# One layer of attention, state-space and expert mixture: the gated unit computed by seven half-size products per slice

## The chip, the cores and the metric

The kernel runs on one core of one Trainium2 chip. The metric is the device time of one execution in microseconds. A core has a matrix engine (PE, with its weight loads listed as PEld), a Vector engine (DVE), a Scalar engine (ACT), GpSimd (POOL) and a queue engine (SP) that here issues most DMA transfers. The on-chip memory is SBUF ("ring", "arena", "small" in the names below), and matrix results land in eight PSUM banks of 128 by 512 float32 ("bank").

## The reference, cut to what matters

256 tokens of width 1024 pass through one layer. The part that the change touches is the second branch and its merge with the first:

```
y = s5_ssm(u, ...)                                    # 256 x 512
zg = gelu(y) @ w_glu + b_glu                          # 512 x 2048
ssm_branch = zg[..., :1024] * sigmoid(zg[..., 1024:])
mixed = sigmoid(gate_a) * attn_branch + sigmoid(gate_s) * ssm_branch
x = x + mixed @ w_out                                 # 1024 x 1024
x = x + moe_swiglu(rmsnorm(x), ...)                   # 32 experts, top 4, 1024 x 2048 and 1024 x 1024 each
x = x + sigmoid(rmsnorm(x) @ w_ple_gate) * rmsnorm(p @ w_ple_proj)
```

All is float32. All 32 experts' weights, about 403 MB, are read once.

## The kernel before, in words

Everything is written out by hand, engine by engine, with semaphores between them; no scheduler moves anything. Weights pass through a ring of nine places of 2 MB. The SP queue issues their loads in one fixed order, each behind a wait for the place to be read out: the input projection (eight pieces), the attention branch, the gated unit (`("glu", 0)` and `("glu", 1)`, places 4 and 5), the output projection (`("out", 0)` and `("out", 1)`, places 6 and 7), and then the experts' pieces. Places 0, 1, 2, 8 and parts of others serve as working memory before the experts' pieces reach them. PSUM banks are handed out by one list of jobs, `order_of_banks`: a job takes the next bank once `free` says that the bank's last job has been read, and its product is announced by `full`.

The stage of the change lies between the last state-space product (job `y3`) and the output projection:

- **The gated unit (L1728).** A place holds 512 columns of the linear half and the 512 matching columns of the gate half. Job `glu{i}` (i from 0 to 7) fills one bank: 128 columns of the linear half for 256 tokens, and 128 of the gate half. A weight block of 128 by 128 is the stationary operand and `GY[:, k, :]`, 256 tokens wide, streams past it; four k are summed.
- **Its eviction.** The Scalar engine takes the sigmoid of the gate half into `SZ` (L793), Vector adds the bias and multiplies (L1167), multiplies with the branch's gate (`tt`, L961) and adds the attention branch (L1171). `mixed_set` counts the eight column blocks.
- **The output projection (L1736)** is already a seven-product scheme. Four blocks of `mixed` and four of the weights are combined: `M_SUM` on Vector (L1175 to L1180) and `W_SUM` on GpSimd (L675 to L680). Six products of 512 columns go into `outa`, `outb`, `outc`, the seventh into `out3` and `out4`. Vector adds each finished sum to `X2` (`add_product`, L1263).
- **Behind it** the second RMSNorm, the transposes (L1748), the router (L1756 to L1767, `choose`), the gather (L1784, L1787) and the first expert's up product (L1911).

A waiting instruction holds up what is behind it on its own engine only. The waits on SP that matter here: place 4 is loaded anew when `glu3` is done, place 5 when `glu7` is done, the halves of places 6, 8 and 7 as the output's products finish one by one, and the second expert's pieces (`BEHIND`) as the first expert's products read out the ring (`head_read`).

Of the kernel before, what the change touches and what calls it, by code (L numbers as in the profile page):

```python
# [5 lines left out]
P = 128  # L6
# [44 lines left out]
def order_of_banks():  # L51
# [8 lines left out]
    jobs += [f"glu{i}" for i in range(8)]  # L60
# [5 lines left out]
def hybrid_layer(nc, x, p, g_mix, w_in, g_q, g_k, w_attn, a_re, a_im, log_dt, b_re, b_im, c_re, c_im, d_skip,  # L66
# [19 lines left out]
    with ExitStack() as ctx:  # L86
# [33 lines left out]
        def spread(ap, n):  # L120
# [40 lines left out]
        SZ = area(A_X, 4, SEQ)  # L161
# [7 lines left out]
                 for at in (6, 7)]  # L169
# [61 lines left out]
        EYES2 = small[:, 448:448 + E]  # L231
# [9 lines left out]
                 "cos_times_set sin_times_set keep_set weight_set weight_full back_set gelu_set sz_set mixed_set x_again "  # L241
                 "glu_gate_in x2_sq x2_ms x2_root x2_normal xn_set xn_half w_sum m_sum prod_full prod_read router_in router_set partial_full partial_set slots_set top_set exp_set chosen_set sel_first_set "
# [19 lines left out]
                     ("glu", 0): "glu3", ("glu", 1): "glu7", ("out", 0): "out4", ("out", 1): "out4"}  # L262
# [90 lines left out]
        def turn_tables(eng, st, lo, n, tmp_at, tmp_last_at):  # L353
# [7 lines left out]
            for level in range(LEVELS):  # L361
# [7 lines left out]
                if level == LEVELS - 1:  # L369
# [6 lines left out]
                    eng.wait_ge(S["cos_times_set"], n)  # L376
                    st.did(eng.tensor_tensor(c1, c1, tmp, ALU.subtract))
                    eng.wait_ge(S["sin_times_set"], n)
# [43 lines left out]
        def _(sp):  # L422
# [63 lines left out]
            for i in (2, 0, 1, 3, 4, 5, 6, 8, 7):  # L486
                at = spot(0, i)
                piece = expert_source(i // PER_EXPERT, i % PER_EXPERT)
                if divmod(i, PER_EXPERT) in AHEAD:
                    for h in range(2):  # L490
                        at_once = h
                        if at == TURN["out", 0][0]:
                            if h == 0:
                                sp.wait_ge(S["prod_full"], 1)
                                sp.wait_ge(S["w_sum"], 4)
                            else:
                                wait_full(sp, "outb")
                        elif at == PLACES - 1:
                            sp.wait_ge(S["prod_full"], 2 + h)
                        elif h == 0:  # L500
                            wait_full(sp, "outc")
                            at_once = 1
# [8 lines left out]
                elif at in held:  # L511
                    wait_full(sp, held[at])
                if i == 3:
# [95 lines left out]
        def _(pool):  # L609
# [51 lines left out]

            wait_full(pool, "y3")
            for t in range(TB):
# [8 lines left out]
            for c in range(2):  # L672
                at, use = TURN["out", c]
                pool.wait_ge(arrived[at], 16 * (use + 1))
            pool.tensor_tensor(W_SUM[0], OUT_W[1][0], OUT_W[0][0], ALU.subtract).then_inc(S["w_sum"], 1)  # L675
            pool.wait_ge(S["w_sum"], 1)
            pool.tensor_tensor(W_SUM[1], OUT_W[1][1], W_SUM[0], ALU.subtract).then_inc(S["w_sum"], 1)
            pool.tensor_tensor(W_SUM[2], OUT_W[1][1], OUT_W[1][0], ALU.subtract).then_inc(S["w_sum"], 1)
            pool.wait_ge(S["w_sum"], 3)
            pool.tensor_tensor(W_SUM[3], OUT_W[0][1], W_SUM[1], ALU.subtract).then_inc(S["w_sum"], 1)  # L680
# [25 lines left out]
        def _(act):  # L706
# [47 lines left out]
            def last_level(table, done):  # L754

                act.wait_ge(S["pool_tables_set"], 1)
                for i in range(TILES):
                    act.activation(table[:, i, P:2 * P], table[:, i, 0:P], ACT.Copy, scale=AKC[:, i:i + 1]).then_inc(S[done], 1)

            BESIDE = {0: "u0", 1: "u1", 3: "g0", 5: "g1"}  # L760
            for s in range(PAIRS + 2):
# [8 lines left out]
                if s == 2:  # L770
                    last_level(COS, "cos_times_set")
                elif s == 3:
                    last_level(SIN, "sin_times_set")
# [15 lines left out]
            for i in range(DT):  # L789
                wait_full(act, f"glu{i}")  # L790
                if i >= 4:
                    act.wait_ge(S["mixed_set"], i - 3)
                act.activation(SZ[:, i % 4, :], ps(f"glu{i}")[:, SEQ:2 * SEQ], ACT.Sigmoid,  # L793
                               bias=PAR2[:, P_BGLU + DT + i:P_BGLU + DT + i + 1]).then_inc(S["sz_set"], 1)


            act.wait_ge(S["mixed_set"], DT)
# [9 lines left out]
            def squared(t, cols, to):  # L807
                act.activation(JUNK[:, cols], X2[:, t, cols], ACT.Square,
                               accum_out=SSQ[:, to:to + 1]).then_inc(S["x2_sq"], 1)

            def normal(t):
                act.wait_ge(S["x2_ms"], t + 1)
# [1355 lines left out]
```

## Time and profile before

| | us |
|---|---|
| median of 3 runs | 1154.44 (1154.4 to 1156.12) |
| the profiled execution's own time | 1154.22 |
| its span, first to last instruction | 1152.5 |
| PE busy in the span | 1111.7 (96%) |
| Vector, Scalar, GpSimd busy | 392.2, 171.3, 167.6 |
| moved by DMA | 440.38 MB, mean 382 GB/s |

The 1.7 us between span and time lie around the program and are taken as fixed. The chain of work that ended last is 71% PE and 26% DMA.

### The profile page before, as it was taken

How to read it: one execution, taken by the hardware profiler on the slowest of the kernel's cores; microseconds unless marked ns; L12 is line 12 of the kernel's file. 1: busy time of each engine (PE TensorE's matmuls, PEld its weight loads, DVE VectorE, ACT ScalarE, POOL GpSimd, SP SyncE). 2: the span in 40 equal slices, each digit the busy share in tenths (PEclk: the TensorE clock that was granted, in tenths of full speed). 3: DMA queues.
4: the chain of work that ended last, by engine and by line, in shares of the span. 5: the costliest groups of instructions: out<-in, count | busy, mean ns of one | idle time of the engine just before them, and what ended most of it. 6: DMA issues, size and time to landing. Idle time of an engine off the chain costs nothing.

```text
span 1152.5 us, 15678 instructions
## 1 busy us (share of the span) xinstructions
PE 1111.7 (96%) x6441; PEld 489.3 (42%) x6441; DVE 392.2 (34%) x831; ACT 171.3 (15%) x319; POOL 167.6 (15%) x187
## 2 busy tenths in 40 slices
PE   9999999999999999998999999999999999999998
PEld 4578886534333333333333333333333333333344
DVE  6558867523222222222232232121212222122226
ACT  2360112500000000000211111111111111010113
POOL 2988992100000000000000000000000000000005
PEclk9999999999999999999999999999999999999999
DMA  9934287899999999999999999999999999999991
GB/s 317 371 104 142 101 327 273 287 410 427 427 426 434 430 432 432 426 437 430 426 437 431 427 434 433 426 436 433 425 436 431 428 435 432 428 435 425 427 420 44
DMA packets 42929, 440.38 MB, mean 382 GB/s; under 512 B 9877, under 2 KB 10449, under 8 KB 24722
## 3 DMA queue, kind: packets, MB, share of 16 engines
q1 hardware_dynamic: 42306, 438.36, 90.9%
q0 software_dynamic: 480, 1.57, 0.4%
q8 instruction: 21, 0.34, 0.1%
q14 instruction: 10, 0.08, 0.0%
q10 hardware_dynamic: 112, 0.02, 0.0%
HBM read 438.89 MB, written 1.05 MB: 382 GB/s over the span
## 4 chain that ended last, share of the span: by engine, by line
PE 71%; DMA 26%; DVE 1%; issue 0%; ACT 0%; SPq 0%; DVEq 0%
PE bank L1911 26%; DMA ring<-in_w_up_dram 18%; PE bank L1965 14%; DMA ring<-in_w_down_dram 9%; PE bank L1558 7%; PE bank L1984 4%; PE bank L1575 4%; PE bank L1875 2%; PE bank L1728 2%; PE bank L1736 2%; PE bank L1776 2%; PE bank L2094 2%; PE bank L1948 1%; PE bank L2022 1%; PE bank L1952 0%
## 5 line engine op out<-in xcount | busy, mean ns | idle before, releaser
L1911 PE MATMUL bank<-ring,arena 128*64 128x512 f32 x2040 | 455.6, 603 | 17.8 <-DMA ring<-in_w_up_dram 17.6
L1911 PEld LDWEIGHTS bank<-ring,arena 128*64 128x64 f32 x2040 | 144.6, 139 | 323.5 <-issue 292.3
L1965 PE MATMUL bank<-ring,arena 128*64 128x512 f32 x1024 | 228.5, 599 | 12.4 <-DMA ring<-in_w_down_dram 11.2
L1352 DVE TENSOR_TENSOR arena<-arena,bank 128x512 f32<-128x512 f32 x128 | 79.5, 682 | 282.1 <-PE bank L1984 282.0
L1328 DVE TENSOR_SCALAR arena<-bank 128x512 f32<-128x512 f32 x32 | 22.1, 692 | 358.4 <-PE bank L1911 358.4
L694 POOL TENSOR_TENSOR ring<-ring 128x2048 f32<-128x2048 f32 x1 | 4.5, 4547 | 910.1 <-DMA ring<-in_w_ple_gate_dram 910.1
L1965 PEld LDWEIGHTS bank<-ring,arena 128*64 128x64 f32 x1024 | 74.0, 137 | 146.3 <-issue 139.2
L884 ACT ACTIVATE arena<-arena 128x512 f32<-128x512 f32 x32 | 20.2, 631 | 498.3 <-DVE arena L1328 498.3
L1558 PE MATMUL bank<-arena,ring 128*128 128x256 f32 x384 | 85.9, 382 | 0.0
L1558 PEld LDWEIGHTS bank<-arena,ring 128*128 128x128 f32 x384 | 72.0, 190 | 12.4 <-issue 3.1
L1984 PE MATMUL bank<-arena 64*128 64x512 f32 x256 | 63.5, 614 | 0.0
L1875 PEld LDWEIGHTS bank<-arena 128*128 128x128 bf16 x1488 | 45.1, 98 | 25.2 <-issue 25.2
L889 ACT ACTIVATE arena<-bank 128x512 f32<-128x512 f32 x32 | 19.1, 597 | 234.8 <-PE bank L1965 234.8
L1875 PE MATMUL bank<-arena 128*128 128x64 bf16 x1488 | 48.8, 193 | 0.0
L1575 PE MATMUL bank<-ring,arena 128*128 128x512 f32 x96 | 42.2, 595 | 0.0
L1984 PEld LDWEIGHTS bank<-arena 64*128 64x128 f32 x256 | 22.2, 186 | 40.2 <-issue 40.2
L1776 PE MATMUL bank<-arena 32*64 32x512 f32 x256 | 34.8, 613 | 0.0
L887 ACT ACTIVATE arena<-bank 128x256 f32<-128x256 f32 x64 | 21.1, 381 | 48.7 <-PE bank L1948 48.7
L1728 PE MATMUL bank<-arena,ring 128*128 128x256 f32 x128 | 27.9, 380 | 0.0
L1575 PEld LDWEIGHTS bank<-ring,arena 128*128 128x128 f32 x96 | 17.9, 190 | 21.6 <-issue 21.0
L1728 PEld LDWEIGHTS bank<-arena,ring 128*128 128x128 f32 x128 | 24.2, 190 | 3.7 <-issue 0.4
L2094 PE MATMUL bank<-ring 128*128 128x512 f32 (+1 forms) x64 | 24.5, 542 | 0.0
(278 smaller groups left out, 807.1 us busy)
## 6 DMA issues: line engine op xcount, KB each, us to landing
ring<-in_w_up_dram SPq DMA_DIRECT2D x40, 4096.0 KB, 33.2
ring<-in_w_down_dram SPq DMA_DIRECT2D x24, 4096.0 KB, 33.3
ring<-in_w_up_dram SPq DMA_DIRECT2D x38, 2048.0 KB, 25.9
ring<-in_w_down_dram SPq DMA_DIRECT2D x14, 2048.0 KB, 15.1
ring<-in_w_up_dram SPq DMA_DIRECT2D x19, 1024.0 KB, 7.7
ring<-in_w_in_dram SPq DMA_DIRECT2D x7, 2048.0 KB, 18.2
ring<-in_w_glu_dram SPq DMA_DIRECT2D x4, 1024.0 KB, 6.3
ring<-in_w_out_dram SPq DMA_DIRECT2D x2, 2048.0 KB, 8.2
```

The source lines that it names most:

```text
L1328: dve.tensor_scalar(ACTS[:, 0, :], bank[UG][:, :], LIMIT, None, ALU.min).then_inc(m["g_set"], 1)
L1352: dve.tensor_tensor(part, part, bank[at][:, :], ALU.add).then_inc(m["sc_add"], 1)
L1558: last = pe.matmul(b[:, SEQ * i:SEQ * (i + 1)], weight(key, a)[:, k, P * m:P * (m + 1)], rhs[:, k, :], start=(k == 0), stop=(k == n - 1))
L1575: last = pe.matmul(b[:, :], HT[:, k, t * P:(t + 1) * P], weight(("in", n), DT)[:, k, :], start=(k == 0), stop=(k == DT - 1))
L1728: last = pe.matmul(b[:, SEQ * h:SEQ * (h + 1)], held[:, k, h, P * (i % 4):P * (i % 4 + 1)], GY[:, k, :], start=(k == 0), stop=(k == WT - 1))
L1736: last = pe.matmul(b, of[:, k, :], w[:, k, cols], start=start and k == 0, stop=stop and k == 3, skip_group_check=True)
L1776: pe.matmul(bank[UG + w][HALF * h:HALF * (h + 1), :], PICK[rows, :], BUP[rows, :], start=True, stop=False)
L1875: last = pe.matmul(bank[GX][:, CAP * d:CAP * (d + 1)], XB[t][:, part, P * d:P * (d + 1)], SELB[:, t, :], start=(i == 0), stop=(i == 3 * TB ...
L1911: last = pe.matmul(to, XS[:, k, :], columns, start=False, stop=(k == DT - 1))
L1965: last = pe.matmul(bank[YB][HALF * c:HALF * (c + 1), :], ACTT[:, j, HALF * h:HALF * (h + 1)], piece[:, j, 512 * c:512 * (c + 1)], start=(h ...
L1984: pe.matmul(bank[at][:, :], WSELT[rows, t, :], Y[rows, :], start=True, stop=True).then_inc(m["sc_full"], 1)
L2094: last = pe.matmul(b, of[:, k, :], w[:, k, cols], start=start and k == 0, stop=(k == 3), skip_group_check=True)
```

## The change: what it does, and the diff

The gated unit is computed by seven products of half-size blocks instead of eight. For each slice s (one place, 512 linear and 512 gate columns) the rows of `y` are halved (the contraction's k = 0, 1 and k = 2, 3), the tokens are halved, and the columns are split in linear and gate. Sums of weight blocks, `G_SUM`, are made on GpSimd, sums of blocks of `y`, `Y_SUM`, on Vector. Each product covers 512 columns and 128 tokens: four column blocks of two k, so the stream past a stationary block is 128 wide instead of 256. The results pile up in the banks `ga`, `gb`, `gc`, `gd` per slice; between products the Scalar engine copies partial sums out (`held`), and Vector adds them (`linear_first`, `gate_first`, `gate_second`). The gate is opened in place in the bank (`opened`, four sigmoids of 128 columns on Scalar, one multiply on Vector), and bias, gate and attention branch are joined in the bank (`joined`, four instructions, and `mixed`). Three of the four blocks of the mixed branch stay in banks; Scalar copies them to `GATE` for the products.

Beside that: GpSimd's sums for the output come later and in another order; the re-read of x and of a bias (DMAs of GpSimd's queue) come behind the eight new sums; the load of place 4 and 5 waits for `gc0` and `gc1` (each slice's last read of its ring place by PE) and for GpSimd's last sums; the unit columns `EYES` are made before the attention; the slot numbers (`SLOT`, `LOGIT`, `RANK`, `pick`) are made behind the output's first evictions. Some semaphores are merged, which changes no order.

```diff
-    jobs += [f"glu{i}" for i in range(8)]
+    jobs += ["gc0", "gc1", "gd0", "ga0", "gd1", "gb0", "gb1", "ga1"]
...
+                    if at in (4, 5):
+                        sp.wait_ge(S["w_sum"], G_SUMS + at - 5)
...
+            for s in range(2):
...
+                glu_sum(0, s, glu_block(s, 0, 1), glu_block(s, 0, 0))
             wait_full(pool, "y3")
+            for s in range(2):
+                glu_sum(1, s, glu_block(s, 1, 1), G_SUM[0][s])
+            for s in range(2):
+                glu_sum(2, s, glu_block(s, 1, 1), glu_block(s, 0, 1))
+            for s in range(2):
+                pool.wait_ge(S["prod_full"], 3 + s)
+                glu_sum(3, s, glu_block(s, 1, 0), G_SUM[1][s])
...
+            for s in range(2):
+                linear_first(s)
+            for s in range(2):
+                gate_first(s)
+            opened("gc0", 0, 0, 1)
+            joined("gb0", 0, 0)
+            gate_second(0)
+            mixed("gb0", 0, 0)
+            gate_second(1)
+            opened("gc1", 1, 0, 2)
+            joined("gb1", 1, 0)
+            mixed("gb1", 1, 0)
+            opened("gd0", 0, 1, 3)
+            joined("ga0", 0, 1)
...
+            opened("gd1", 1, 1, 4)
+            joined("ga1", 1, 1)
+            mixed("ga1", 1, 1)
...
+            def turned_product(job, w, of, start=True):
+                b = take(job) if start else ps(job)
+                for m in range(4):
+                    for k in range(2):
+                        last = pe.matmul(b[:, P * m:P * (m + 1)], w[:, k, P * m:P * (m + 1)], of[:, k, :],
+                                         start=start and m == 0 and k == 0, stop=(k == 1), skip_group_check=True)
+                return last
...
+            for s in range(2):
+                pe.wait_ge(S["w_sum"], 7 + s)
+                wait_full(pe, f"gd{s}")
+                done(turned_product(f"ga{s}", G_SUM[3][s], y_block(1, 1), start=False), f"ga{s}")
```

**On PE**, the gated unit's end and the output's first product. Before, L1728 stands in eight pieces, one for each bank (the order counts a float32 product once; the trace lists it as two records, each with its weight load); bank0 is `glu6`, bank1 `glu7`, bank2 `outa`:

```order
L1728 MATMUL bank0<-arena,ring 128x256 [waits free0]
L1728 MATMUL bank0<-arena,ring 128x256 x7
L1728 MATMUL bank1<-arena,ring 128x256 [waits free1]
L1728 MATMUL bank1<-arena,ring 128x256 x7
L1736 MATMUL bank2<-ring,arena 128x512 [waits mixed_set,arrived6,free2]
```

After it, L1861 stands in fourteen pieces of eight; here are the last five and the output's first (bank5 is `ga0`, bank1 `ga1`, bank3 `gc1`, bank2 `outa`):

```order
L1861 MATMUL bank3<-arena,ring 128x128 [waits prod_read]
L1861 MATMUL bank3<-arena,ring 128x128 x7
L1861 MATMUL bank5<-arena,ring 128x128 [waits prod_read,w_sum,m_sum]
L1861 MATMUL bank5<-arena,ring 128x128 x7
L1861 MATMUL bank1<-arena,ring 128x128 [waits prod_read,w_sum]
L1861 MATMUL bank1<-arena,ring 128x128 x7
L1861 MATMUL bank5<-arena 128x128 [waits full4,w_sum]
L1861 MATMUL bank5<-arena 128x128 x7
L1861 MATMUL bank1<-arena 128x128 [waits full6,w_sum]
L1861 MATMUL bank1<-arena 128x128 x7
L1906 MATMUL bank2<-ring,arena 128x512 [waits mixed_in,arrived6,free2]
```

Sixty-four products of 256 columns became 112 of 128, and the last two groups wait for what Vector writes (`full4`, `full6` are `gd0` and `gd1`).

**On Vector**, before, from the last gated block to the sums for the output (bank1 is `glu7`):

```order
L1167 SCALAR_TENSOR_TENSOR arena<-bank1,small,arena 128x256 [waits sz_set]
L961 TENSOR_TENSOR arena<-arena 128x256 [waits free1]
L1171 TENSOR_TENSOR arena<-arena 128x256 [waits dve_step]
L1175 TENSOR_TENSOR arena<-arena 128x512 [waits mixed_set]
L1177 TENSOR_TENSOR arena<-arena 128x512 [waits m_sum]
L1178 TENSOR_TENSOR arena<-arena 128x512
L1180 TENSOR_TENSOR arena<-arena 128x512 [waits m_sum]
```

After it, from the opened gate of `gc0` to those sums (bank7 is `gb0`, bank0 `gb1`, bank1 `ga1`):

```order
L1273 TENSOR_TENSOR arena<-bank2,arena 128x4x128 [waits sz_set]
L1281 SCALAR_TENSOR_TENSOR bank7<-bank7,small,arena 128x128 [waits free2]
L1281 SCALAR_TENSOR_TENSOR bank7<-bank7,small,arena 128x128 x3
L1267 TENSOR_TENSOR bank4<-bank5,arena 128x512 [waits prod_full,free4]
L1287 TENSOR_TENSOR bank7<-bank7,arena 128x512 [waits dve_step]
L1267 TENSOR_TENSOR bank6<-bank1,arena 128x512 [waits prod_full,free6]
L1273 TENSOR_TENSOR arena<-bank3,arena 128x4x128 [waits sz_set]
...
L1314 TENSOR_TENSOR arena<-bank7,arena 128x512 [waits mixed_in,mixed_set,free5]
L1316 TENSOR_TENSOR arena<-arena,bank1 128x512 [waits mixed_in]
L1318 TENSOR_TENSOR arena<-arena,bank7 128x512 [waits m_sum]
L1320 TENSOR_TENSOR arena<-bank0,arena 128x512 [waits m_sum]
```

All of these read at least one operand from a bank, where before the sums for the output (L1175 to L1180) read both from the arena; between `gc0` and the sums stand twelve more instructions of 128 columns and eight more of 512, left out here.

**On GpSimd**, what stands between the last state and the output's sums, after the change:

```order
L675 TENSOR_TENSOR arena<-ring 128x1024 [waits glu_gate_in,arrived4,back_set]
L675 TENSOR_TENSOR arena<-ring 128x1024 [waits glu_gate_in,arrived5]
L675 TENSOR_TENSOR ring<-ring,arena 128x1024 [waits w_sum,full1]
L675 TENSOR_TENSOR ring<-ring,arena 128x1024 [waits w_sum]
L675 TENSOR_TENSOR ring<-ring 128x1024 x2
L675 TENSOR_TENSOR arena<-ring 128x1024 [waits prod_full,w_sum] x2
L694 DMA arena<-in_x_dram 128x1024 x2
L700 DMA arena<-in_b_up_dram 32x1024 [waits full0,free1]
L700 DMA arena<-in_b_up_dram 32x1024 x3
L701 IOTA arena 128x256
L707 TENSOR_TENSOR ring<-ring 128x2048 [waits w_sum,prod_full,arrived7,arrived6]
```

Eight sums of 1024 elements now stand ahead of the DMAs and of the four sums for the output; before, the DMAs came right behind the last state.

## Rows read from the trace of the kernel before

**Rows 1.** The page: the span in 40 slices, DMA busy in tenths
```profile
DMA  9934287899999999999999999999999999999991
```
**Rows 2.** Windows: PE, PEld, DVE, ACT, POOL busy, granted clock, DMA share, GB/s
```profile
180.00:185.00 5.00, 5.00 (x24) 4.29 (x23) 4.72 (x13) 0.84 (x3) 0.00 (x0) 1.00 0.00 0
...
210.00:215.00 5.00, 4.51 (x47) 3.12 (x46) 3.39 (x15) 2.27 (x6) 1.45 (x3) 1.00 0.36 96
...
220.00:225.00 5.00, 5.00 (x28) 1.95 (x26) 1.92 (x7) 0.60 (x3) 0.00 (x0) 1.00 0.72 261
225.00:230.00 5.00, 5.00 (x28) 1.59 (x24) 3.41 (x12) 3.32 (x3) 0.00 (x0) 1.00 1.01 364
```
**Rows 3.** Timeline of SP, the issuing queue: start, length, line, transfer
```profile
171.05 14.14 SPq L441 DMA_DIRECT2D ring<-in_w_down_dram  x2
...
220.75 0.35 SPq L540 DMA_DIRECT2D ring<-in_w_up_dram  x1
```
**Rows 4.** The chain that ended last: start, length, what
```profile
157.01 27.82 PE bank L1728 x128
184.84 20.60 PE bank L1736 x48
...
487.93 34.19 DMA ring<-in_w_up_dram
```
**Rows 5.** Chain, PE and PEld timelines, and the page's row of L1728's loads
```profile
53.26 0.87 PE bank L1625 x8
...
217.07 1.42 PEld L1787 LDWEIGHTS bank<-arena 128*128 128x128 f32 x12 [0.34 <-DVE arena L1247]
...
205.27 1.11 PE L1748 MATMUL bank<-ident,arena 128*128 128x128 f32 x8
...
L1728 PEld LDWEIGHTS bank<-arena,ring 128*128 128x128 f32 x128 | 24.2, 190 | 3.7 <-issue 0.4
```
**Rows 6.** Timeline of POOL; the last row is from the page's DMA issues
```profile
61.44 2.35 POOL L356 TENSOR_TENSOR ring<-ring,arena 128x1024 f32<-128x1024 f32 x1
...
152.78 2.80 POOL L646 TENSOR_TENSOR ring<-ring,arena 128x256 f32<-128x256 f32 x4
...
158.61 1.96 POOL L670 DMA_DIRECT2D arena<-in_b_up_dram  x4
...
160.88 4.53 POOL L675 TENSOR_TENSOR ring<-ring 128x2048 f32<-128x2048 f32 x1
...
arena<-in_x_dram POOLq DMA_DIRECT2D x2, 512.0 KB, 11.1
```
**Rows 7.** Timeline of DVE: start, length of all, line, shape
```profile
52.42 1.28 DVE L1093 TENSOR_TENSOR arena<-arena,bank 128x512 f32<-128x512 f32 x2 [4.34 <-PE bank L1575]
...
144.45 0.69 DVE L961 TENSOR_TENSOR bank<-bank,ring 128x512 f32<-128x512 f32 x1
...
157.08 0.48 DVE L1128 SCALAR_TENSOR_TENSOR arena<-arena,small,bank 128x256 f32<-128x256 f32 x1 [0.35 <-PE bank L1643]
...
161.82 3.88 DVE L961 TENSOR_TENSOR arena<-arena 128x256 f32<-128x256 f32 x1
165.74 4.63 DVE L1171 TENSOR_TENSOR arena<-arena 128x256 f32<-128x256 f32 x1
...
188.31 0.69 DVE L1177 TENSOR_TENSOR arena<-arena 128x512 f32<-128x512 f32 x1
188.92 0.69 DVE L1178 TENSOR_TENSOR arena<-arena 128x512 f32<-128x512 f32 x1
...
205.47 1.28 DVE L1263 TENSOR_TENSOR arena<-arena,bank 128x512 f32<-128x512 f32 x2 [0.45 <-PE bank L1736]
...
209.78 0.25 DVE L1228 SCALAR_TENSOR_TENSOR arena<-bank,small 128x32 f32<-128x32 f32 x1 [0.35 <-PE bank L1765]
```
**Rows 8.** Timeline of ACT
```profile
70.70 0.60 ACT L780 ACTIVATE arena<-bank 128x512 f32<-128x512 f32 x1 [2.60 <-PE bank L1558]
...
142.94 0.72 ACT L788 ACTIVATE arena<-arena 128x256 f32<-128x256 f32 x2
```

More of the change, by code:

```diff
@@ new lines, in gate_first, with gate_second @@
+            def gate_first(s):
+                wait_full(dve, f"gc{s}")
+                dve.wait_ge(S["prod_read"], 5 + s)
+                b = ps(f"gc{s}")[:, :]
+                dve.tensor_tensor(b, b, HELD_A[s], ALU.add).then_inc(S["zg_set"], 1)
+            def gate_second(s):
+                at, use = BANKS[f"gd{s}"]
+                dve.wait_ge(free[at], use)
+                dve.wait_ge(S["prod_full"], 7 + s)
+                dve.tensor_tensor(ps(f"gd{s}")[:, :], ps(f"ga{s}")[:, :], HELD_C[s], ALU.add).then_inc(full[at], 1)
@@ new lines, in opened, with joined @@
+            def opened(job, s, t, n):
+                dve.wait_ge(S["sz_set"], n)
+                part = branch_part(1, s, t)
+                release(dve.tensor_tensor(part, quarters(job), part, ALU.mult), job)
+                released(dve, job)
+            def joined(job, s, t):
+                for m in range(4):
+                    part = ps(job)[:, P * m:P * (m + 1)]
+                    i = P_BGLU + 4 * s + m
+                    st.did(dve.scalar_tensor_tensor(part, part, PAR2[:, i:i + 1], GATE[:, DT + 4 * s + m, P * t:P * (t + 1)],
+                                                    ALU.add, ALU.mult))
@@ new lines, in glu_block, with y_block @@
+            def glu_block(s, r, c):
+                return GLU_W[s][:, 2 * r:2 * r + 2, c, :]
+            def y_block(t, r):
+                return GY[:, 2 * r:2 * r + 2, P * t:P * (t + 1)]
+            pe.wait_ge(S["gelu_set"], 2)
+            pe.wait_ge(S["glu_gate_in"], 32)
+            for s in range(2):
+                arrive(("glu", s))
+                turned_product(f"ga{s}", glu_block(s, 0, 0), y_block(0, 0)).then_inc(S["prod_full"], 1)
+            pe.wait_ge(S["gelu_set"], WT)
+            for s in range(2):
+                done(turned_product(f"gb{s}", glu_block(s, 1, 0), y_block(0, 1)), f"gb{s}")
@@ new lines, in _ @@
+            pe.wait_ge(S["m_sum"], 1)
+            for s in range(2):
+                pe.wait_ge(S["w_sum"], 1 + s)
+                turned_product(f"gc{s}", G_SUM[0][s], Y_SUM[0]).then_inc(S["prod_full"], 1)
+            pe.wait_ge(S["m_sum"], 2)
+            for s in range(2):
+                pe.wait_ge(S["w_sum"], 3 + s)
+                pe.wait_ge(S["prod_read"], 1 + s)
+                turned_product(f"ga{s}", G_SUM[1][s], Y_SUM[1], start=False).then_inc(S["prod_full"], 1)
+            pe.wait_ge(S["m_sum"], 3)
@@ new lines, in _ @@
+            for s in range(2):
+                pe.wait_ge(S["prod_read"], 3 + s)
+                done(turned_product(f"gc{s}", glu_block(s, 1, 1), Y_SUM[2], start=False), f"gc{s}")
+            pe.wait_ge(S["m_sum"], Y_SUMS)
+            for s in range(2):
+                pe.wait_ge(S["w_sum"], 5 + s)
+                pe.wait_ge(S["prod_read"], 5 + s)
+                turned_product(f"ga{s}", G_SUM[2][s], Y_SUM[3], start=False).then_inc(S["prod_full"], 1)
+            for s in range(2):
+                pe.wait_ge(S["w_sum"], 7 + s)
+                wait_full(pe, f"gd{s}")
+                done(turned_product(f"ga{s}", G_SUM[3][s], y_block(1, 1), start=False), f"ga{s}")
```

241 lines of the change are left out of this document (148 added, 93 removed).

## The prediction

> **What bounds the kernel now.** I read the page first. DMA is at 9 tenths or more from the ninth slice to the last but one, and well below in the slices from 58 to 144 us [rows 1]. Then the windows of the middle: from 180 to 185 no byte moves while PE is busy throughout, from 210 to 215 DMA is busy for 0.36 of the time, from 220 to 225 for 0.72, and from 225 on for all of it [rows 2]. So until about 225 us the transfers wait for PE, and behind it the queue is never empty. The timeline of SP says by what: its issue at 220.75 is the first that waits for the first expert's products, and in the pair issued from 171.05 on, the second (place 5) waits until the gated unit is done [rows 3]. The chain agrees: it runs over PE alone through L1728 and L1736 and meets its first long DMA piece at 487.93 [rows 4]. The experts' stream is one unbroken transfer whose start is the moment at which PE opens it. Whatever PE gains or loses before 220 us should therefore reach the end one for one, and what DMA gains between 171 and 210 is given back in its idle time of 210 to 215.
>
> The gated unit is 27.82 us of that chain, from 157.01 to 184.84, then 20.60 us of output products to 205.44 without a wait [rows 4].
>
> **Products on PE.** Removed: 128 records of 256 columns, 217 ns apart (27.82 / 128). Added: 7 products x 2 slices x 8 = 112 float32 products, 224 records of 128 columns. By half the stream's width they would be 109 ns apart, but each record also has a weight load of 128 by 128, and that does not shrink. The nearest rows: L1625, transposes with 128 columns and contiguous operands, 0.87 / 8 = 109 ns apart; L1787, real float32 products with the same weight shape and 64 columns, whose twelve loads begin (1.42 - 0.19) / 11 = 112 ns apart; L1748, 128 columns with strided weights, (1.11 - 0.28) / 7 = 118 ns (0.19 and 0.28 are the last one's own length) [rows 5]. A load takes 190 ns by its own length, but its pace is that of L1787. The new weights are contiguous; I take 111 ns: 224 x 0.111 = 24.9 us, with 24.4 (109) and 26.4 (118) as the bounds. **That is 2.9 us less** (3.4 to 1.4), if nothing waits: the unit then ends at 181.9. A product is 1.78 us.
>
> A rule of the Trainium skill speaks against it: "TensorE: Matmul & The Clock Gate", section "The mechanism" of its part on packing, says that weight loads overlap matmuls in flight only when their row groups differ. By that rule load and stream of each record would follow one another, and the time would be that of the last case of rival 5 instead of the forecast. The trace does not agree: the full-height loads of L1625 hide behind streams of 128 columns.
>
> **Sums on GpSimd.** Eight sums of 1024 elements; a row of that size took 2.35 us. They begin when the last state is done, 152.78 + 2.80 = 155.6 [rows 6], so the four pairs are ready at 160.3, 165.0, 169.7 and 174.4. PE, going from 157.0 in pairs of 3.55 us, needs the first sum of each pair at 164.1, 167.7, 174.8 and 178.3. Each first sum is ready 2.3 us ahead of its pair, so the cover is 4.5 us or more everywhere. Costed at nothing. Behind them come six DMA issues (four took 1.96 us; 3.2 for all) and the slot numbers, so the four output sums of 4.53 us [rows 6] end at about 182.5, 187.1, 191.7 and 196.2; PE wants them at 188.8, 192.2, the last but one in `out3`, and the last at 199.1. The cover is 2.9 us at the least. x now lands by 174.4 + 11.1, some 186 [rows 6]; Vector wants it at 190. Places 4 and 5 are loaded from about 173 to 175 on, which fills the idle 180 to 185 and then has no one waiting.
>
> **Row sums on Vector.** Four adds of 256 elements with both operands in the arena. Here the trace has a warning: the two such adds of 161.82 and 165.74 took 3.88 and 4.63 us, and each ended when a GpSimd sum of 4.53 us ended (the first 160.88 + 4.53 = 165.41) [rows 6, 7]. The new ones start at 158.1 and will each wait for the GpSimd sum in progress: done at 160.6, 162.9, 165.3, 167.6, against needs of 164.1, 167.7, 171.2, 174.8. Cover 3.5 us or more. Costed at nothing.
>
> **Evictions: the chain that decides.** Operations with one operand in a bank do not wait for GpSimd: the multiply at 144.45 took 0.69 while GpSimd was busy [rows 7]. So I count by length. A 512-wide one: 0.69, so 0.61 apart where independent (188.31 to 188.92), about 0.71 where dependent. A 128-wide one with scalar: between 0.25 (32 wide, 209.78) and 0.48 (256 wide, 157.08), so 0.35, 0.28 apart; four of them 1.2 us [rows 7]. Scalar copies take 0.60, and four sigmoids 1.15 (two of 256 took 0.72) [rows 8]. `gc1` is whole at 174.8, so Vector ends `gate_first(1)` at 175.5. From there it is never idle: four `opened` (2.8), four `joined` (4.8), two `gate_second` (1.2), four adds of the attention branch (2.9), then M_SUM[2] and M_SUM[0] (1.4): 13.1 us, to 188.6. PE needs M_SUM[0] behind two products of 3.43 (20.60 / 6), at 181.9 + 6.9 = 188.8. **The margin is 0.2 us.** On the way, `gate_second(0)` comes at 178.1 and PE wants it at 178.3; `gate_second(1)` at 179.4, wanted at 180.1. I take no wait, but each 0.1 us more on a 512-wide step costs some 1.2 us, and `joined` at 1.6 us instead of 1.2 costs 1.6 us.
>
> **Waits added.** PE's last two groups wait for Vector (`gd0`, `gd1`), and the whole output stands behind them. GpSimd's last two sums wait for `gc0` and `gc1` (165.9 and 167.7, before GpSimd gets there), with the DMAs of x behind them. SP's load of place 4 waits for the seventh sum (172.1) and `gc0` (173.0), with every expert's piece behind it; the next such pieces wait for the output's products anyway.
>
> **Moved.** The unit columns go into Vector's idle 4.34 us ahead of 52.42 [rows 7], where four small adds fit even if each waits for a GpSimd step: nothing. The slot numbers and the first pick (some 0.6 us) now stand ahead of the norm's scalars; the adds behind them had 0.45 us of idle time [rows 7], which covers most: 0.1 us lost.
>
> **Sum.** 27.8 - 24.9 = 2.9 gained, no new wait, 0.1 lost: 2.8. The profiled execution took 1154.2, 0.2 under the median, so 1151.4 against it and **1151.5 us** on the scale of the median of 1154.44, 0.25% faster.
>
> **Rivals.**
> 1. *Forecast* (47%): unit in about 24.9, waits under 0.6 us in all; 1151.0 to 1152.1.
> 2. *Vector's eviction chain becomes the bound* (27%): its steps a tenth of a microsecond longer, or `joined` near four times 0.40. PE then waits for `gd0` or, more, ahead of `outc` for M_SUM[0]. For it: the chain has no idle time, the margin is 0.2. Against: each step is costed from a row. 1 to 2.8 us of the gain go: 1152.5 to 1154.3.
> 3. *The pace is 118 ns* (8%): the strided row holds for contiguous weights too. 224 x 0.118 = 26.4, and Vector starts later with it: 1.4 us gained, 1153.0.
> 4. *The gain is hidden* (8%): the stream's start hangs on a transfer and not on PE. Against: the idle DMA of 210 to 225 [rows 2]. About 1154.4.
> 5. *Slower by weight loads* (10%, with what is like it): the loads set the pace. From 134 ns on (30 us for the unit) the kernel is slower by 0.2%; if a load can't begin before the last ended, at 190 ns [rows 5], the unit takes 42.6 us and the kernel 1169; if load and stream can't overlap at all (112 + 109 = 221 ns, 49.5 us), it takes 1176 (2% of the 10). For it: that is the one thing that seven half-size products don't shrink, 224 loads in place of 128. Against: L1787's loads are as long and 112 ns apart. A smaller case is a chain on Vector 5.3 us longer than counted (18.4 for 13.1), as it would be if GpSimd's four long sums held up even half of a dozen steps by 1 us each: 1157.
>
> **How the numbers follow.** The likeliest is case 1. From 1150.8 (pace 109, no wait) to 1154.9 lies all but case 5 and a little at both ends: 1150.8 to 1154.9. Case 1's own range is 1150.8 to 1152.1. A run can tell about 0.2%, 2.3 us, from no change. Faster by more (under 1152.1): case 1 and a bit of 2 and 3, 0.50. Within: 2, 3, 4 and the rest, 0.39. Slower: 0.11.
>
> **What would show it.** L1861 in 24.4 to 25.5 us, 109 to 114 ns apart; no idle PE ahead of the last two groups; the output's 48 records again in 20.6 us, ahead of the third product nothing or under 0.5 us; the transposes beginning near 202.5; the first `head_read` issue near 217.9; four row sums each of 2 us and more. Wrong if L1861's loads come 130 ns apart or if PE idles for Vector ahead of `outc` by over 1 us.

## The result, and the profile after

The changed kernel took **1159.58 us** (median of 6 runs, 1158.78 to 1159.82) against 1154.63 for the kernel before (6 runs, 1153.92 to 1156.12). The ratio is 1.0041, with an interval of [1.003, 1.0052]: slower by 0.4%. The forecast was 1151.5 in a range of 1150.8 to 1154.9, so the time lies outside the range and on the other side. The profiled execution took 1159.76, with a span of 1158.0 (1152.5 before).

The chain of the changed kernel stands against [rows 4] (start, length, what):

```profile
158.30 11.51 DVE arena L1232
...
169.86 20.84 PE bank L1861 x160
190.69 20.60 PE bank L1906 x48
211.30 0.94 PE bank L1918 x8
...
224.67 3.65 PE bank L2084 x16
...
493.85 33.52 DMA ring<-in_w_up_dram
```

Before, the chain ran over PE alone here. Now it leaves PE for 11.51 us for one small Vector add, L1232, the first of the new row sums. The output's first product starts at 190.69, where it started at 184.84. That is 5.85 us late. The output itself takes 20.60 as before. From its end to the first expert's products it is 211.30 to 224.67, 13.37 us. Before it was 205.44 to 218.77, 13.33:

```profile
218.77 3.65 PE bank L1911 x16
```

The long DMA piece starts 5.92 us late. So the loss is made between 157 and 191 us, and nearly all of it reaches the end: the spans of the two profiled executions differ by 5.5 us, the medians by 4.95.

PE's timeline of the same stretch (start, length of all, line, shape, count, idle time before and who ended it):

```profile
157.10 7.41 PE L1861 MATMUL bank<-arena,ring 128*128 128x128 f32 x64
169.86 6.54 PE L1861 MATMUL bank<-arena 128*128 128x128 f32 x32 [5.34 <-DVE arena L1232]
176.24 10.88 PE L1861 MATMUL bank<-arena,ring 128*128 128x128 f32 x96
186.96 3.74 PE L1861 MATMUL bank<-arena 128*128 128x128 f32 x32
190.53 20.77 PE L1906 MATMUL bank<-ring,arena 128*128 128x512 f32 x48
```

The first four products (64 records) go at (7.41 - 0.27) / 63 = 113 ns, 0.27 being a record's own length; the 96 at (10.88 - 0.27) / 95 = 112. Then there are two losses. PE idles 5.34 us for L1232, and the 32 records behind the idle time take 6.54 us where the last 32 take 3.74. The windows say why:

```profile
165.00:170.00 5.00, 0.14 (x1) 0.14 (x1) 4.97 (x2) 0.00 (x0) 4.52 (x2) 0.87 0.60 254
170.00:175.00 5.00, 5.00 (x24) 5.00 (x25) 2.23 (x5) 0.60 (x1) 1.21 (x1) 0.50 0.01 3
175.00:180.00 5.00, 5.00 (x44) 5.00 (x44) 0.00 (x0) 1.19 (x2) 4.59 (x4) 0.94 0.01 2
```

From 170 to 175 the granted clock is 0.50, the 1.2 GHz level, and 24 records fit where 44 do at 0.94. PE had been idle from 164.5 to 169.9; the granted clock is 1.00 in the window of 160 to 165 and falls on average to 0.87 within the idle window.

Vector and GpSimd in those microseconds:

```profile
158.30 12.75 DVE L1232 TENSOR_TENSOR arena<-arena 128x256 f32<-128x256 f32 x4 [0.58 <-ACT arena L821]
...
184.91 1.13 DVE L1281 SCALAR_TENSOR_TENSOR bank<-bank,small,arena 128x128 f32<-128x128 f32 x4
...
196.10 0.68 DVE L1316 TENSOR_TENSOR arena<-arena,bank 128x512 f32<-128x512 f32 x1
```

```profile
155.63 4.68 POOL L675 TENSOR_TENSOR arena<-ring 128x1024 f32<-128x1024 f32 x2
160.27 4.66 POOL L675 TENSOR_TENSOR ring<-ring,arena 128x1024 f32<-128x1024 f32 x2
164.87 4.65 POOL L675 TENSOR_TENSOR ring<-ring 128x1024 f32<-128x1024 f32 x2
173.79 2.35 POOL L675 TENSOR_TENSOR arena<-ring 128x1024 f32<-128x1024 f32 x1 [4.27 <-PE bank L1861]
```

The shortest and the longest of the four row sums are in the view of their line:

```profile
L1232 DVE TENSOR_TENSOR arena<-arena x4: 418/424/11501, 158.3 to 170.6; 128x256 f32<-128x256 f32 x4
```

One row sum took 11.50 us, the other three some 0.42 each. It was issued during GpSimd's second weight sum and was done at 169.80, 0.28 us after the sixth sum had ended (164.87 + 4.65 = 169.52). GpSimd passed from sum to sum at about 160.3, 162.6, 164.9 and 167.2, four boundaries, and Vector got in at none of them. It got in at the fifth, where GpSimd had to wait for a product of PE. That product waited in its turn for the row sum. The forecast had taken the next boundary.

The account of the unit, from 157.1 to 190.69: at full pace it would be 25.2 us (224 x 0.1125), the wait adds 5.3, and the lower clock some 2.8 (20.84 for the 160 records behind the wait against 160 / 224 x 25.2 = 18.0). The sum is 33.3, and 33.6 is measured against 27.8 [rows 4].

### The profile page after: what moved, and what is told of

Read it like the earlier page. It is cut to its first block, busy times and chain, and to the rows that moved or that the text cites. A ratio compares the mean times of both kernels' runs of the same rounds, so it can differ in the third digit from the quotient of the medians.

```text
span 1158.0 us, 15939 instructions
## 1 busy us (share of the span) xinstructions
PE 1112.8 (96%) x6537; PEld 492.1 (42%) x6537; DVE 393.7 (34%) x844; ACT 177.0 (15%) x336; POOL 185.7 (16%) x195
## 4 chain that ended last, share of the span: by engine, by line
PE 70%; DMA 27%; DVE 2%; issue 1%; ACT 0%; SPq 0%; DVEq 0%
PE bank L2084 26%; DMA ring<-in_w_up_dram 17%; PE bank L2138 14%; DMA ring<-in_w_down_dram 9%; PE bank L1696 7%; PE bank L2157 4%; PE bank L1713 4%; PE bank L2048 2%; PE bank L1906 2%; PE bank L1946 2%; PE bank L1861 2%; PE bank L2267 2%; PE bank L2121 1%; DVE arena L1232 1%; PE bank L2195 1%
## 5 line engine op out<-in xcount | busy, mean ns | idle before, releaser
L1696 PE MATMUL bank<-arena,ring 128*128 128x256 f32 x384 | 85.9, 382 | 0.0
L1696 PEld LDWEIGHTS bank<-arena,ring 128*128 128x128 f32 x384 | 72.0, 190 | 12.4 <-issue 3.1
L2048 PEld LDWEIGHTS bank<-arena 128*128 128x128 bf16 x1488 | 45.1, 98 | 25.2 <-issue 25.2
L2121 PE MATMUL bank<-ident,arena 128*128 128x128 f32 x128 | 23.9, 309 | 0.6
## 6 DMA issues: line engine op xcount, KB each, us to landing
ring<-in_w_down_dram SPq DMA_DIRECT2D x14, 2048.0 KB, 14.9
```

The source lines that it names most:

```text
L1696: last = pe.matmul(b[:, SEQ * i:SEQ * (i + 1)], weight(key, a)[:, k, P * m:P * (m + 1)], rhs[:, k, :], start=(k == 0), stop=(k == n - 1))
L2048: last = pe.matmul(bank[GX][:, CAP * d:CAP * (d + 1)], XB[t][:, part, P * d:P * (d + 1)], SELB[:, t, :], start=(i == 0), stop=(i == 3 * TB ...
L2121: last = pe.transpose(bank[at][:, P * j:P * (j + 1)], rows[:, 2 * i + j, :], I)
```

## Experiments

The first theory was a hold by GpSimd: it keeps something that a Vector add with two operands outside the banks needs, and frees it only where it stops or waits for its own work to end (in its sharp form: a boundary between two GpSimd instructions without such a wait never lets Vector in). The changed kernel does wait for two of its own sums, ahead of the third for the first and ahead of the fourth for the second, but each of these was already done, so GpSimd did not stop for them. Against the theory stood two others: that PE's wait alone is the whole loss, whatever its cause, and that the small moves (unit columns, slot numbers) have a part in it. Each expectation says in its own words what the letters in it stand for. Line numbers of an experiment with an added line are one or more higher.

### The row sums ahead of the long run of GpSimd sums

```diff
             wait_full(pool, "y3")
+            pool.wait_ge(S["m_sum"], Y_SUMS)
             for s in range(2):
```

> The changed kernel, with one wait added: GpSimd makes its first two weight sums and then waits until Vector's four row sums are done, before it goes on to the other sums. Theory A (the first row sum was held up by GpSimd's unbroken run of six weight sums, PE idled 5.3 us for it and then ran 160 records at a lower granted clock): the row sums are done by about 162.3, PE doesn't idle ahead of its third product, the unit ends near 182.2 instead of 190.5, and the time falls by about 8 us from the changed kernel, to 1151.3 to 1152.5, some 2.6 us under the kernel before. Rival B (the loss came from something else behind the unit, such as transfers that start late): the unit is shorter, but the time stays over 1155.

Measured: 1151.98 us (11 runs, 1151.03 to 1152.77) against 1154.5 for before (24 runs), ratio 0.9978 [0.9969, 0.9987]. It is faster than both kernels, and rival B falls. The chain:

```profile
157.25 25.21 PE bank L1862 x224
182.45 20.60 PE bank L1907 x48
...
216.41 3.65 PE bank L2085 x16
```

Vector's rows:

```profile
158.38 3.54 DVE L1233 TENSOR_TENSOR arena<-arena 128x256 f32<-128x256 f32 x4 [0.58 <-ACT arena L822]
...
187.87 0.68 DVE L1317 TENSOR_TENSOR arena<-arena,bank 128x512 f32<-128x512 f32 x1
...
191.03 1.41 DVE L1396 TENSOR_TENSOR arena<-arena,bank 128x512 f32<-128x512 f32 x2 [0.90 <-DMA arena<-in_x_dram]
```

The unit runs without a gap at 25.21 / 224 = 112.5 ns a record. That is 2.6 us less than before, and the first expert starts 2.4 us earlier than before (216.41 against 218.77). M_SUM[0] (L1317) is ready at 188.55; PE wants it at 182.45 + 6.87 = 189.32. So the eviction chain has 0.8 us of margin and costs nothing. Vector waits 0.90 us for x, off PE's path. The forecast's mechanism holds once the row sums are out of the way.

### A wait for each sum's own end, and PE kept busy

GpSimd waits, ahead of each weight sum, for the end of the one before:

```diff
             for s in range(2):
+                pool.wait_ge(S["w_sum"], s)
                 glu_sum(0, s, glu_block(s, 0, 1), glu_block(s, 0, 0))
...
-                pool.wait_ge(S["w_sum"], 1 + s)
+                pool.wait_ge(S["w_sum"], 2 + s)
                 glu_sum(1, s, glu_block(s, 1, 1), G_SUM[0][s])
             for s in range(2):
+                pool.wait_ge(S["w_sum"], 4 + s)
                 glu_sum(2, s, glu_block(s, 1, 1), glu_block(s, 0, 1))
```

> The changed kernel, but GpSimd waits for the end of each weight sum before it starts the next. It asks what lets Vector in. Theory A1 (Vector gets its turn at a boundary only where GpSimd drains, as at the waits between the output's sums of the kernel before): each row sum waits for one sum of 2.35 us, they are done near 160.7, 163.2, 165.6 and 168.0 (about what was forecast), PE doesn't idle, and the time is 1151.5 to 1153. Rival A2 (Vector is let in only when GpSimd's queue of such work ends): the first row sum still ends near 170, and the time is that of the changed kernel, 1159 or more.

Measured: 1152.17 (10 runs), ratio 0.9981 [0.9972, 0.999].

```profile
158.54 9.97 DVE L1234 TENSOR_TENSOR arena<-arena 128x256 f32<-128x256 f32 x4 [0.58 <-ACT arena L823]
```

The four adds now take 2.5 us each, one for each boundary, as the forecast had it, and PE needs none of them earlier: theory A1 gave that, and rival A2 falls.

The other kernel leaves the hold and gives PE twelve more products, whose result is overwritten, ahead of its wait:

```diff
+            b = take("gc0")
+            for _ in range(12):
+                pe.matmul(b[:, 0:SEQ], glu_block(0, 0, 0)[:, 0, 0:P], GY[:, 0, :], start=True, stop=True)
```

> The changed kernel, with 12 more products of 256 columns on PE just ahead of its wait for the first row sum; their result is overwritten, and they fill about 5.1 of the 5.3 us in which PE idled. It parts the idle time from what the lower clock behind it cost. Theory: the wait itself stays, so the third product still starts near 169.9, but the granted clock stays at 1.0 and the 160 records behind it take about 17.9 us instead of 20.8: time 2.9 us under the changed kernel, 1156.4 to 1157. Rival: the slow records come from the weight loads and not from the clock; they again take near 20.8 us and the time is unchanged, 1159.5, or more.

Measured: 1157.85 (7 runs), ratio to before 1.003 [1.0019, 1.0041]. The span is 1155.3, where the changed kernel's is 1158.0.

```profile
169.84 18.13 PE bank L1861 x160
```

```profile
164.28 5.35 PE L1881 MATMUL bank<-arena,ring 128*128 128x256 f32 x24
169.84 3.84 PE L1861 MATMUL bank<-arena 128*128 128x128 f32 x32 [0.21 <-DVE arena L1232]
173.52 10.88 PE L1861 MATMUL bank<-arena,ring 128*128 128x128 f32 x96
```

```profile
165.00:170.00 5.00, 4.79 (x23) 3.90 (x22) 4.97 (x2) 0.00 (x0) 4.50 (x2) 1.00 0.63 261
170.00:175.00 5.00, 5.00 (x46) 5.00 (x47) 2.21 (x5) 1.19 (x2) 2.96 (x2) 1.00 0.00 0
```

PE goes on at the same moment, 169.84, but with the granted clock at 1.00. The same 32 records take 3.84 us and not 6.54, and the 160 behind the wait 18.13 and not 20.84. The span is 2.7 us shorter although PE did 5.35 us more work. That the wait is the whole loss falls, and so does the rival that the slow records come from the weight loads: in these two traces 5.3 us of the loss behind 164.5 are the wait and 2.7 the clock that it costs. The forecast of the time missed: 1156.4 to 1157 was expected, and the median is 1157.85, 1.7 us under the changed kernel's and not 2.9. The profiled execution is the fastest of the seven; what the others lost elsewhere was not looked for.

### The hold measured by itself

Two kernels that compute nothing of the layer: GpSimd does a run of subtractions of 1024 elements (2048 in three of the cases), and Vector adds of 256 elements, on other tiles, beside them. The first differs in whether GpSimd waits for its own sums:

```python
if j and drained:
    pool.wait_ge(summed, total[i] + j)
pool.tensor_tensor(to, a, b, ALU.subtract).then_inc(summed, 1)
```

> A small kernel of its own that computes nothing of the layer. In seven phases GpSimd subtracts blocks (both operands in SBUF) while Vector makes six dependent adds of 256 elements with both operands in SBUF: (SINGLE) six of 1024 with no wait between them; (DRAINED) the same with a wait for the one before; (LONG) four of 2048, with a wait only ahead of the third; (INPLACE) the same, each over its own second operand; (LONGDRAINED) 2048, a wait before each; (PAIRS) 1024, a wait before every second; (BANK) as SINGLE, but Vector's first operand in PSUM. Theory A1: in SINGLE the first add lasts about 6 x 2.3 = 14 us, in DRAINED each lasts 2.3, in PAIRS 4.6, in BANK 0.4. LONG is open: by the kernel before (an add got in between two sums of 2048 with no wait) 4.6 each; if the wait alone decides, 9.2. Rival A2: DRAINED looks like SINGLE.

```profile
42.36 14.95 DVE L96 TENSOR_TENSOR small<-small 128x256 f32<-128x256 f32 x6 [40.95 <-POOL mark L71]
57.50 14.94 DVE L96 TENSOR_TENSOR small<-small 128x256 f32<-128x256 f32 x6 [0.19 <-POOL mark L71]
72.63 19.52 DVE L96 TENSOR_TENSOR small<-small 128x256 f32<-128x256 f32 x6 [0.19 <-POOL mark L71]
...
146.89 2.72 DVE L96 TENSOR_TENSOR small<-acc,small 128x256 f32<-128x256 f32 x6 [0.19 <-POOL mark L71]
```

Without waits (42.36) and with them (57.50) it is 14.9 us for six adds, 2.5 each. Vector got in at every boundary, and at every boundary of sums twice as long (72.63). The three cases left out, two with 2048 and one with a wait ahead of every second sum, took 19.52, 19.52 and 14.94. With one operand in a bank (146.89) it isn't held at all. The sharp form of the theory, that a boundary without a wait never lets Vector in, fell here. The kernel before had one such case already. Its GpSimd makes the second and third of the output's sums with no wait between them, and the last wait stands one boundary earlier:

```profile
165.49 4.59 POOL L677 TENSOR_TENSOR ring<-ring 128x2048 f32<-128x2048 f32 x1
170.04 4.70 POOL L678 TENSOR_TENSOR ring<-ring 128x2048 f32<-128x2048 f32 x1
```

The add of 165.74 got in between them and was done at 170.37 [rows 7]. The adds' and sums' views, a later start of the adds, and waits that are already met were next:

```python
PHASES = {"PLAIN": (), "POOLCUT": (CUT,), "VECCUT": (VCUT,), "BOTHCUT": (CUT, VCUT), "CUTDRAINED": (CUT, VCUT, DRAIN),
          "SATISFIED": (SATISFIED,)}
```

> A second small kernel that computes nothing of the layer. The first one let Vector in at every boundary, with or without a wait on GpSimd, so the missing wait alone doesn't explain the 11.5 us. Here GpSimd makes six sums of 1024 in each of six phases, Vector's four adds of 256 arrive during the second sum as in the changed kernel, and the shapes are those of the changed kernel one by one: PLAIN (one run of elements on both), POOLCUT (GpSimd reads blocks of 512 with gaps), VECCUT (Vector reads blocks of 128 with gaps), BOTHCUT, CUTDRAINED (BOTHCUT with a wait before each sum), SATISFIED (PLAIN with waits that are already met). Theory C (the gapped shape on GpSimd keeps the port over a boundary): POOLCUT and BOTHCUT show a first add of some 11.5 us, PLAIN, VECCUT, SATISFIED and CUTDRAINED show 2.5 us each. Rival D (the gapped shape on Vector): VECCUT and BOTHCUT are the long ones. Rival E (the late arrival): PLAIN is long too. If all are 2.5 us, the cause lies in something else of the big kernel.

```profile
44.72 9.87 DVE L96 TENSOR_TENSOR small<-small 128x256 f32<-128x256 f32 x4 [44.72 <-POOL plain L79]
59.41 9.91 DVE L96 TENSOR_TENSOR small<-small 128x256 f32<-128x256 f32 x4 [4.82 <-POOL poolcut L79]
...
118.43 9.91 DVE L96 TENSOR_TENSOR small<-small 128x256 f32<-128x256 f32 x4 [4.82 <-POOL satisfied L79]
```

All six cases lie between 9.87 and 10.03 us for four adds. None of these makes the hold.

### The small moves alone

The kernel before, with the unit columns early and the slot numbers and first pick behind the evictions, as in the changed one:

```diff
+            st.did(dve.memset(EYES[:, E:], 0.0))
+            st.link(dve.tensor_tensor(EYES[:, 0:E], ident[:, 0:E], ident[:, E:2 * E], ALU.add))
...
-            pick(M, 0)
...
+            st.did(dve.tensor_copy(SLOT, SLOT_I))
...
+            pick(M, 0)
```

> The kernel before, with only the unit columns made ahead of the attention and the slot numbers behind the output's evictions, as in the changed kernel. Theory: no change, within 0.1% of 1154.5; the stretch from the first transpose behind the output to the first expert's product takes 13.3 to 13.4 us. Rival: the moved work lies on the path and costs its 0.6 us or more there.

Measured: 1154.84 (10 runs) against 1154.93 for before (13 runs), ratio 0.9999 [0.999, 1.0009]: no change. From the first transpose to the first expert's product it is 13.35 us (205.62 to 218.97). They have no measurable part in the loss.

### One wait: midway, ahead, and a memset in its place

Since whole runs of waits weren't needed in the small kernels, what does one wait do in the changed kernel? Theory **F**: the hold goes over boundaries only in a run of GpSimd work that reaches back, without a wait for its end, into the state-space work; one such wait anywhere ahead of the boundary ends it. Rival **G**: each boundary of the real kernel needs its own wait.

```diff
             wait_full(pool, "y3")
+            pool.wait_ge(S["w_sum"], 2)
             for s in range(2):
```

> The changed kernel, with GpSimd waiting once, for the end of its second weight sum, ahead of the third; the sums behind it have no such wait, as in the changed kernel. Theory F (GpSimd holds the port over a boundary only in a run of work that goes back, without such a wait, to the state-space work before it; one wait clears that): all four row sums take about 2.5 us each, the last ends near 168.5, PE doesn't idle, 1151.5 to 1153. Rival G (in this kernel only a boundary with a wait lets Vector in): the first row sum ends near 160.8 and the other three only near 170, PE idles some 2 us ahead of its fourth product, 1153.5 to 1155.

```diff
             pool.wait_ge(S["back_set"], 2 * TILES)
+            pool.wait_ge(S["state_set"], 2 * TILES)
             for s in range(2):
```

> The changed kernel, with GpSimd waiting once, for the end of the last state's fold, ahead of its first weight sum; six sums follow with no wait for one another, and the first row sum arrives during the second. Theory F (a wait clears the run): row sums of 2.5 us each, PE doesn't idle, 1151.5 to 1153. Rival G (only a wait right at the boundary lets Vector in): the first row sum again takes some 11.5 us and the time is again 1159 or more.

Midway, one run took 1152.47, with a span of 1150.7. Ahead, it took 1152.0 (10 runs, 1151.48 to 1152.73), ratio 0.9978 [0.9968, 0.9987], and a span of 1150.0. GpSimd and Vector with the wait ahead:

```profile
155.80 4.67 POOL L675 TENSOR_TENSOR arena<-ring 128x1024 f32<-128x1024 f32 x2
160.44 5.02 POOL L675 TENSOR_TENSOR ring<-ring,arena 128x1024 f32<-128x1024 f32 x2
165.42 5.03 POOL L675 TENSOR_TENSOR ring<-ring 128x1024 f32<-128x1024 f32 x2
```

```profile
158.31 9.92 DVE L1233 TENSOR_TENSOR arena<-arena 128x256 f32<-128x256 f32 x4 [0.58 <-ACT arena L822]
```

One wait, which costs GpSimd 0.17 us or less (155.63 against 155.80), clears the hold at all four boundaries behind it. None of these has a wait for the sum right before it; the two waits for earlier sums are there as in the changed kernel, and already met. The two pairs beside the adds take 5.02 and 5.03 us where they took 4.66 and 4.65: the price of letting Vector in is readable on GpSimd's side. G falls. Midway, the four adds took 9.84 us together.

Is it the wait, or would anything between the two kinds of work do? A small probe gave GpSimd a history of its own before the sums, with the state-space work's shapes: a run of long subtractions, twelve small multiplies and adds, the same with a wait behind them, and with Vector busy on a bank.

```python
PHASES = ("CHAIN", "SMALL", "SMALLSYNC", "SMALLBUSY")
```

> A third small kernel that computes nothing of the layer, to make the long hold by itself. Six sums of 1024 on GpSimd with no waits in each of four phases, and Vector's four adds arrive during the second; what differs is what GpSimd does ahead without a wait: (CHAIN) six more sums of 1024; (SMALL) twelve instructions as the state-space stage has them, multiplies of 512 by a repeated table and adds of 256; (SMALLSYNC) the same, and a wait for their end ahead of the sums; (SMALLBUSY) as SMALL, with Vector at work beside it on a bank. Theory F: at least SMALL or SMALLBUSY shows a first add of some 10 us, SMALLSYNC 2.5 us. If all show 2.5 us, GpSimd's history alone doesn't make it.

```profile
53.80 9.88 DVE L110 TENSOR_TENSOR small<-small 128x256 f32<-128x256 f32 x4 [52.40 <-POOL to_chain L89]
79.89 9.91 DVE L110 TENSOR_TENSOR small<-small 128x256 f32<-128x256 f32 x4 [16.20 <-POOL to_small L89]
...
132.18 9.98 DVE L110 TENSOR_TENSOR small<-small 128x256 f32<-128x256 f32 x4 [4.95 <-POOL to_smallbusy L89]
```

Again 2.5 us an add in all of them. Then the changed kernel itself, with a memset of one column and no wait, at the place of the wait ahead and at that of the wait midway:

```diff
+            pool.memset(MARK_POOL, 0.0)
             for s in range(2):
```

> The changed kernel with one more GpSimd instruction and no wait: a memset of one column, ahead of the first weight sum, where the kernel with one wait had the wait. Theory F1 (it is the wait for the end of the earlier GpSimd work that lets Vector in at later boundaries; another instruction does nothing): the first row sum takes about 11.5 us again, PE idles 5.3 us, time near 1159.6. Theory F2 (any instruction of another kind between the state-space work and the sums breaks the run): four row sums of about 2.5 us, PE doesn't idle, time near 1152.

> The changed kernel with a memset of one column, and no wait, ahead of the third weight sum. By F1: as the changed kernel, first row sum about 11.5 us, time near 1159.6. By F2: the row sums get in at the memset's boundary, at about 160.3, and at those behind it, 2.5 us each; time near 1152. A memset ahead of the sums that does not help together with one midway that does would mean that Vector gets in only at a boundary with an instruction of another kind, and then each of the later row sums should be long instead.

They took 1158.6 and 1158.28 (one run each; before on the same chip 1155.65). With the memset ahead:

```profile
155.75 0.11 POOL L678 MEMSET small<- 128x1 f32 x1
155.80 4.68 POOL L675 TENSOR_TENSOR arena<-ring 128x1024 f32<-128x1024 f32 x2
160.44 4.66 POOL L675 TENSOR_TENSOR ring<-ring,arena 128x1024 f32<-128x1024 f32 x2
```

```profile
158.44 12.78 DVE L1233 TENSOR_TENSOR arena<-arena 128x256 f32<-128x256 f32 x4 [0.58 <-ACT arena L822]
```

The hold is there in full in both (12.78 and 12.83 us for the four adds), and PE idles 5.37 and 5.42. So it is the wait that ends the hold, and an instruction of another kind does not. Waits that were already met did not end it either, since the changed kernel has two. What isn't parted is whether GpSimd must wait for its own work or whether any short stop would do: the wait ahead also makes GpSimd pause for up to 0.17 us, and the memset doesn't.

Both kernels are 1.0 to 1.3 us faster than the changed one, with one run each. In their traces the lower clock was shorter. With the memset ahead, the 160 records behind the wait took 19.58 us and not 20.84, and the window from 170 to 175 has a granted clock of 0.69 and not 0.50:

```profile
170.00:175.00 5.00, 4.98 (x31) 4.98 (x32) 2.39 (x5) 0.60 (x1) 1.33 (x1) 0.69 0.01 3
```

## Why the prediction was wrong

**The step that failed** is the one on the row sums: "The new ones start at 158.1 and will each wait for the GpSimd sum in progress: done at 160.6 ... Cover 3.5 us or more. Costed at nothing." The first was done at 169.8 and not at 160.6, and PE, which needed it at 164.5, stood idle for 5.3 us. The step had the right pair of engines and the right class of operation, and it had the warning of [rows 6, 7] in hand. It read from two adds that "each ended when a GpSimd sum of 4.53 us ended", and took the *next* boundary for a rule. The trace of before had no case of a Vector add that meets a run of GpSimd sums directly behind the state-space work, because DMA issues and the slot numbers stood between ([rows 6]: 158.61). The wait was bounded from one side only. A bound from the other side, the end of all GpSimd work that is ready (169.5), would have given PE idle from 164.5 on, and a time near 1157 as a rival with a mechanism.

The Trainium skill, "SBUF — State Buffer", section "Who interferes with whom", says that a Vector `tensor_tensor` with both inputs in SBUF contends with GpSimd's reads. The same page of the Trainium skill, section "SBUF: two separate sides", says that whichever of the two starts first keeps the shared ports for its whole instruction and the other fully blocks. The runs agree for one instruction: 2.5 us an add in the three kernels with a wait of GpSimd for its own work and in every small probe with sums of 1024, and no block with an operand in a bank. They don't agree with "instruction" as the unit in the changed kernel, where the block went over four boundaries.

**The second cost, not priced at all**, is the clock. Every row of before near here had it at 1.00 [rows 2], and the forecast's cases with idle PE counted idle time alone. Here 5.3 us of idle PE cost 2.7 us more, shown by the trace with PE kept busy; by the medians it is 1.7, and in the two traces with a memset about 1.5 (19.58 and 19.62 against 18.13).

**Rival 5** gave 1157 for a Vector chain held up by GpSimd's sums. It is near the size by luck: it put the wait in the eviction chain, which wasn't held. That chain took 12.5 us (184.28 to 196.78) for a forecast of 13.1, with `joined` at 1.13 for 1.2. Rival 2 (27%) fell: margin 0.8 us in the run with row sums first. Rival 3 (118 ns) and the loads as the bound fell: 112 ns. Rival 4 (the gain is hidden) fell too: in the run with row sums first the unit's gain of 2.6 us came out as 2.5 in the median.

**What held.** The pace was 111 ns by forecast and is 112 to 113, so the unit is 25.2 us against 24.9. The mean load is 192 ns long in the run with row sums first and still starts every 112.5 ns behind streams of 128 columns. The rule of the section "The mechanism" in the Trainium skill's "TensorE: Matmul & The Clock Gate", that weight loads overlap matmuls in flight only when their row groups differ, does not hold for these full-height loads, as the forecast took it. The output took 20.60 again. A gain or loss ahead of 220 us reaches the end nearly one for one, in both directions: +5.85 at the output's start is +5.9 at the long DMA piece and +5.5 in the span, and -2.4 (182.45 against 184.84) is -2.5 in the median. The small moves cost nothing measurable (0.1 us by forecast). The sum of the gain, 2.8, is 2.3 to 2.6 in the kernels without the hold that have ten runs or more, at 1152.0 to 1152.2 for a forecast of 1151.5.

**What stays open** is what in GpSimd's state-space work makes the later boundaries closed. That the wait opens them is shown, by a wait ahead, one midway and one at each sum against two memsets. The history that the small probes gave it, with its kinds of instructions, shapes and a busy Vector, isn't enough by itself: they never showed a hold. That work also has waits on other engines and DMA traffic around it, and neither was tried. Nor was a stop of GpSimd for another engine, ahead of the run, in place of the wait for its own work.

## What to carry to other kernels

Price a Vector operation with both inputs outside the banks, issued beside a run of GpSimd operations, up to the end of all GpSimd work that is ready, not to the end of one operation; then look who waits for it. If it is on the path, put one wait of GpSimd for the end of the work directly ahead of the run, or the Vector work ahead of the run: either turned +0.4% into -0.2% here. A wait for something already done was no help. A wait on PE of some 5 us cost 1.5 to 2.7 us more in the clock behind it here, so a rival with idle PE needs that term.

## What the runs showed of the hardware

- A Vector add of 0.42 us was held 11.50 us, over four GpSimd boundaries. With one wait of GpSimd for its own last instruction ahead of the run, it and its successors took 2.5 us each. A memset in the wait's place, and waits already met, changed nothing.
- A GpSimd pair of sums took 4.64 to 4.69 us where it let nobody in and 4.84 to 5.05 in the kernels where an add got in at each boundary: a sign by which the two are told apart in a timeline.
- The same stall cost PE's clock differently from one profiled execution to the next: 0.50 over 170 to 175 us in the changed kernel and 0.69 in its twin with a memset, with idle times of 5.34 and 5.37 us. The unit's end differs by 1.1 us (190.69 and 189.60) for it. Whether this hangs on the kernel or on the run isn't shown, with one trace of each.
